# Second attention of a two-layer encoder step: biased scores written to on-chip memory, and unread products on the matrix engine

## The chip, the cores and the metric

The kernel runs on one core of a Trainium2 chip. What is compared is the device time of one execution in microseconds (us), from the runs of the kernel before and of the changed kernel on the same chip. Five engines work side by side and meet only through semaphores: TensorE (PE in the profile, PEld for its weight loads), VectorE (DVE), ScalarE (ACT), GpSimd (POOL) and SyncE (SP, which starts the transfers). Each engine takes its own instructions in the order in which the program lists them.

## The reference, cut to what matters

Two layers are computed for 512 prompt tokens and 32 sample tokens (544 columns together). Each layer projects its normalised input, runs two groups of attention heads, projects their outputs, and ends with a gated feed-forward part. The change touches the second attention alone ("B"): 8 heads of width 64; each query looks only at keys chosen by an indexer, with a bias by relative position.

```python
logits = jnp.einsum('bqhd,bqkhd->bqhk', qb, ks).astype(jnp.float32) * dh ** -0.5
bias = rel_bias[t5_bucket(sel_pos - pb[None, :, None])].astype(jnp.float32)
logits = logits + jnp.swapaxes(bias, 2, 3)
logits = jnp.where(valid[:, :, None, :], logits, -jnp.inf)
p = jax.nn.softmax(logits, axis=-1)
return jnp.einsum('bqhk,bqkhd->bqhd', p.astype(vs.dtype), vs)
...
x = x + jnp.concatenate([o_a.reshape(B, T, WIDTH_A), o_b.reshape(B, T, WIDTH_B)], axis=-1) @ w_out
```

The kernel computes full score rows and pushes the keys that were not chosen far below with an added mask.

## The kernel before, in words

Activations lie with features on the partitions and the 544 tokens along the free axis. Every weight block of 128 columns (a "unit", such as `bk` 3: keys of the second attention, head pair 3) is multiplied by TensorE in two halves of 24 products each (`("G", kind, i, 0)` and `("G", kind, i, 1)`, lines 1171, 1172 and 1175: weights and activations are each split in a high and a low part, three products per pair, 272 columns a product). ScalarE makes the high part of a unit (L887) as soon as the unit two before it is multiplied, and GpSimd then makes the low part (L1690).

One list of steps, written out by `layer_steps`, `a_phase` and `b_phase`, is walked by every engine; each engine executes what is its own in each step, in the order of the list. The second attention has 34 tiles of scores: for each of the four head pairs, four blocks of 128 queries (128, 256, 384, 512 keys wide) and two heads, then two tiles for the sample tokens. Two tiles make a pair, and step j of `b_phase` (j from 0 to 17) holds, in this order:

- `BL j`: TensorE writes the scores of pair j to two banks of its accumulator memory (PSUM), `a_ps[0]` and `a_ps[1]` (L1371; L1373 adds the mask). VectorE adds the bias in place and takes the row maxima (L1666), and negates them (L1668). Semaphore `b_max` says that a tile's maximum is there.
- `BX`: ScalarE takes the exponentials from `a_ps` into `prob` in on-chip memory (SBUF), with the row sums (L1020). Semaphore `b_exp`.
- work that fills the step: `N` (sums of squares for the key or query norm, L1210, read by VectorE at L1454), `Y` and `M` (the reciprocal root on ScalarE and VectorE), `W` (the normed queries or keys, L1498 and L1509 to L1511), `T` (transposes for the outputs), `G` (the next units: `bk`, `bq`, `bv`, and in steps 13 and 15 the first halves of the output projection, `wo` 0 and 1), `BR` (VectorE inverts the sums, L1673; GpSimd scales the probabilities, L1704; semaphore `b_nrm`).
- `BV p` in steps 5, 9, 13, 17: the product with the values for head pair p, into `a_ps[3]` (L691). VectorE copies the result out (L760).
- `BT`, one step late: TensorE transposes the two tiles of pair j-1 into `a_ps[2]` (both tiles, for the two narrow blocks) or into `a_ps[2]` and `a_ps[3]` (L1388; semaphore `bt_full`), and ScalarE copies them to `wts` and `work` (L1038, L1040; semaphore `bt_out`). On ScalarE these copies stand behind the exponentials of pair j.
- on VectorE then part of the top-k search of the sample tokens (L734, L737), or from step 9 the split of the first attention's output (`O`, L1051 and L1679).

After step 17 follow `BV s` (L1402, 24 narrow products for the sample tokens), the `O` steps 4 to 7, and the second half of `wo` 0 (`("G", "wo", 0, 1)`), which waits for them.

Two waits order the scores on TensorE in the kernel before: `BL j` waits until the exponentials of pair j-1 are done, since those still read `a_ps[0]` and `a_ps[1]`:

```python
pe.wait_ge(b_exp.sem, b_exp.at(l, btiles[2 * j - 1]))
```

and where a head pair begins (j = 4, 8, 12), also until `W` has written its keys. On ScalarE each exponential waits for the transposes (`bt_full`) of the tile four before, whose place in `prob` it takes.

Of the kernel before, what the change touches and what calls it, by code (L numbers as in the profile page):

```python
# [33 lines left out]
ALU = mybir.AluOpType  # L34
ACT = mybir.ActivationFunctionType
# [9 lines left out]
KT = DM // P  # L45
PAIRS = NH // 2
QB = SEQ // P
# [68 lines left out]
    return [("G", kind, i, 0), ("G", kind, i, 1)]  # L116


B_TILES = [(2 * p + e, b) for p in range(PAIRS) for b in range(QB) for e in range(2)] + [("s", 0), ("s", 1)]


# [42 lines left out]
def b_phase():  # L164


    n = len(B_TILES) // 2
    first, half, after = ({j: [] for j in range(n + 1)} for _ in range(3))
    for q in range(PAIRS - 1):
        p, j = q + 1, QB * q  # L170
        k = product("bk", p)
        first[j] += [("N", "bq", p), ("BR", j), ("Y", "bq", p), ("M", "bq", p)]
        half[j] += [k[0]] if q else []
        after[j] += [("W", "bq", p)]
        first[j + 1] += [("BR", j + 1)]
        half[j + 1] += [k[1], ("E", "bk", p)]
        after[j + 1] += [("S", "bk", p)]
        first[j + 2] += [("N", "bk", p), ("BR", j + 2), ("Y", "bk", p), ("M", "bk", p)]
        first[j + 3] += [("T", "bk", p - 1), ("BR", j + 3), ("W", "bk", p)]
        if p < PAIRS - 1:  # L180
            later = product("bq", p + 1)
            half[j + 2] += [later[0]]
            half[j + 3] += [later[1], ("E", "bq", p + 1)]
            after[j + 3] += [("S", "bq", p + 1)]
    last = QB * (PAIRS - 1)
    value = product("bv", PAIRS - 1)
    half[last - 1] += [value[0]]
    half[last] += [value[1], ("E", "bv", PAIRS - 1)]
    first[last] += [("T", "bk", PAIRS - 1)]
    first[last + 1] += [("T", "bv", PAIRS - 1)]  # L190
    half[last + 1] += [("G", "wo", 0, 0)]
    half[last + 3] += [("G", "wo", 1, 0)]
    for j in range(last, n):
        first[j] += [("BR", j)]
    for j in range(9):
        after[j] += [("TOPK", 1)]
    for j in range(KT // 2):
        after[9 + j // 2] += [("O", j)]
    s = []
    for j in range(n + 1):  # L200
        if j < n:
            s += [("BL", j), ("BX", 2 * j), ("BX", 2 * j + 1)]
        s += first[j] + half[j]
        if j >= 2 and B_TILES[2 * j - 4][1] == QB - 1:
            s += [("BV", (j - 2) // QB)]
        if j:
            s += [("BT", 2 * j - 2), ("BT", 2 * j - 1)]
        s += after[j]
    s += [("BV", "s")]
    return s  # L210


# [92 lines left out]
def trunk(nc, io, out):  # L305
# [31 lines left out]
    with ctx:  # L337
# [531 lines left out]
        def _(act):  # L869
# [8 lines left out]
            for l, st in steps:  # L878
# [135 lines left out]
                elif k == "BX":  # L1014
                    i = st[1]
                    w = b_width(btiles[i])
                    act.wait_ge(b_max.sem, b_max.at(l, btiles[i]))
                    if i >= 4:
                        act.wait_ge(bt_full.sem, bt_full.at(l, btiles[i - 4]))
                    act.activation(prob[:, i % 4, 0:w], a_ps[i % 2][:, 0:w], ACT.Exp,  # L1020
                                   bias=stat[:, i % 4, 1:2], accum_out=stat[:, i % 4, 2:3]).then_inc(b_exp.sem, 1)
                elif k == "BT":

# [88 lines left out]
        def _(pe):  # L1112
# [15 lines left out]
            for l, st in steps:  # L1128
# [65 lines left out]
                elif k == "R":  # L1194

                    if st[1] == 1:
                        if l:
                            pe.wait_ge(g_free[2].sem, g_free[2].last(l, slot_last[(2, l - 1)]))
                        pe.wait_ge(sqx_done.sem, sqx_done.at(l, st))
                    else:  # L1200
                        pe.wait_ge(b_exp.sem, b_exp.at(l, btiles[-1]))
                        pe.wait_ge(sqx_done.sem, sqx_done.at(l, st))
                    for a in range(2):
                        mm = pe.matmul(a_ps[a][:, 0:HALF], ones, sq[:, 1, a * HALF:(a + 1) * HALF], start=True, stop=True)
# [107 lines left out]
                elif k in ("ASZ", "ASS", "ASV"):  # L1312
# [22 lines left out]
                    else:  # L1335
# [3 lines left out]
                        for p in range(PAIRS):  # L1339
                            for kb in range(SKB):  # L1340
                                r, o = (P, kb * 256) if kb < 2 else (DEC, 512)
                                mm = pe.matmul(a_ps[3][:, p * 64:(p + 1) * 64], vs_nat["a"][0:r, kb, p * P:(p + 1) * P], wts[0:r, o + p * 64:o + (p + 1) * 64],
                                               start=(kb == 0), stop=(kb == SKB - 1))
                        mm.then_inc(o_full.sem, 1)
                elif k == "BL":
                    j = st[1]
                    pair = btiles[2 * j:2 * j + 2]
# [2 lines left out]
                    if j == 0:  # L1350
                        pe.wait_ge(a_w.sem, a_w.at(l, "s"))
                    else:
                        pe.wait_ge(b_exp.sem, b_exp.at(l, btiles[2 * j - 1]))
                    if (0, 1) in pair:
                        pe.wait_ge(tk_done.sem, tk_done.at(l, "p"))
                    if pair[0][0] == "s":
# [51 lines left out]
        def _(dve):  # L1408
# [13 lines left out]
            for l, st in steps:  # L1422
# [233 lines left out]
                elif k == "BL":  # L1656
                    for i in (2 * st[1], 2 * st[1] + 1):
                        t = btiles[i]
                        w = b_width(t)
                        dve.wait_ge(bl_full.sem, bl_full.at(l, t))  # L1660
                        if i >= 4:
                            dve.wait_ge(b_nrm.sem, b_nrm.at(l, btiles[i - 4]))
                        elif l:
                            dve.wait_ge(b_nrm.sem, b_nrm.last(l, btiles[i - 4]))
                        bias = bias_s[:, t[1], :] if t[0] == "s" else strip[:, t[0], SEQ - w:SEQ]
                        dve.tensor_tensor_reduce(a_ps[i % 2][:, 0:w], a_ps[i % 2][:, 0:w], bias, 1.0, TAKEN, ALU.add, ALU.max, stat[:, i % 4, 0:1])  # L1666
                        dve.drain()
                        dve.tensor_scalar(stat[:, i % 4, 1:2], stat[:, i % 4, 0:1], -1.0, None, ALU.mult).then_inc(b_max.sem, 1)  # L1668
                elif k == "BR":
# [79 lines left out]
```

## Time and profile before

| | |
|---|---|
| median of 3 runs | 1685.29 us (1685.22 to 1686.87) |
| profiled execution, its own time | 1682.84 us |
| span of its instructions | 1681.1 us |
| TensorE busy, share of the span | 94% (1586.4 us) |
| VectorE, ScalarE, GpSimd busy | 57%, 41%, 38% |
| mean granted TensorE clock | 0.984 of full speed |

The span runs from the first to the last instruction of the profiled execution; 1.74 us of its own time lie around it. The profile gives, for every instruction, its start and duration, and in brackets how long its engine had idled before it and what ended that. The granted clock is the share of full speed that TensorE had in a stretch; it is 1.00 (2.4 GHz) or 0.50 (1.2 GHz) at each moment. The second attention runs from about 275.6 to 399.5 us in the first layer, and from about 1098.1 to 1218.9 us in the second.

### The profile page before, as it was taken

The page shows a single profiled execution, that of the slowest core. Times are in us where ns is not written, and L with a number is a line of the kernel's source. Part 1 is how long each engine was busy: PE and PEld are TensorE (multiplying, and loading weights), DVE is VectorE, ACT ScalarE, POOL GpSimd, SP SyncE. Part 2 cuts the span into 40 slices and gives each one's busy share as a digit, 9 for nine tenths or more (in the row PEclk, how much of TensorE's full clock was granted, in tenths as well). Part 3 has the DMA queues.
Part 4 walks back from the last instruction along what each step waited for, and adds up shares of the span by engine and source line. Part 5 has one row for each costly group of instructions (what it writes and reads, how often), then busy time and mean ns, then how long its engine had stood idle before and what let it go on. Part 6 is the DMA issues. An engine that isn't in the chain of part 4 may idle for free.

```text
span 1681.1 us, 29872 instructions
## 1 busy us (share of the span) xinstructions
PE 1586.4 (94%) x11754; PEld 1467.2 (87%) x11762; DVE 966.3 (57%) x1764; ACT 683.6 (41%) x1296; POOL 631.6 (38%) x346
## 2 busy tenths in 40 slices
PE   6999998888999999999999999988799999999998
PEld 5788886767999999999987888866699999999998
DVE  6657757753666336516767667666366661662461
ACT  4335453543344234314433354535334431442342
POOL 5223332323643434333552333223264433334432
PEclk9999999998999999999999999999999999999999
DMA  6322211120322333333233322111122333323233
GB/s 187 90 85 84 70 40 38 52 66 26 88 83 82 88 89 89 88 89 89 74 90 109 93 58 58 43 41 45 53 66 87 89 86 91 89 83 89 81 89 94
DMA packets 242178, 131.43 MB, mean 78 GB/s; under 512 B 10302, under 2 KB 236590, under 8 KB 242038
## 3 DMA queue, kind: packets, MB, share of 16 engines
q1 hardware_dynamic: 242038, 129.52, 27.1%
q8 instruction: 93, 1.52, 0.4%
q14 instruction: 47, 0.39, 0.1%
HBM read 117.59 MB, written 11.62 MB: 77 GB/s over the span
## 4 chain that ended last, share of the span: by engine, by line
PE 70%; DVE 14%; ACT 6%; issue 3%; DVEq 3%; POOL 2%; ACTq 1%; DMA 0%; SPq 0%
PE g_ps L1171 13%; PE g_ps L1172 12%; PE g_ps L1175 12%; PE a_ps L1172 7%; PE a_ps L1171 7%; PE a_ps L1175 7%; DVE score L737 1%; ACT work L980 1%; PE a_ps L1264 1%; POOL w_lo L1690 1%; PE a_ps L1250 1%; DVE a_ps L1666 1%; DVE top L734 1%; PE a_ps L691 1%; ACT w_hi L887 1%
## 5 line engine op out<-in xcount | busy, mean ns | idle before, releaser
L1690 POOL TENSOR_TENSOR w_lo<-raw,w_hi 128x1024 fp32r<-128x1024 f32 (+2 forms) x210 | 504.9, 2404 | 712.5 <-ACT w_hi L887 712.5
L1171 PE MATMUL g_ps<-h_hi,w_hi 128*128 128x272 f32 (+1 forms) x1616 | 450.2, 296 | 8.9 <-DVEq L1573 2.9
L1172 PE MATMUL g_ps<-h_lo,w_hi 128*128 128x272 f32 (+1 forms) x1616 | 438.7, 290 | 0.0
L887 ACT ACTIVATE w_hi<-raw 128x1024 fp32r<-128x1024 f32 (+2 forms) x210 | 217.3, 1035 | 453.8 <-PE g_ps L1175 316.7
L1175 PE MATMUL g_ps<-h_hi,w_lo 128*128 128x272 f32 (+1 forms) x1616 | 336.7, 290 | 0.0
L1171 PEld LDWEIGHTS g_ps<-h_hi,w_hi 128*128 128x128 f32 (+1 forms) x1616 | 305.9, 189 | 22.9 <-issue 10.8
L1172 PEld LDWEIGHTS g_ps<-h_lo,w_hi 128*128 128x128 f32 (+1 forms) x1616 | 305.5, 189 | 1.3 <-issue 0.5
L1582 DVE SCALAR_TENSOR_TENSOR wts<-work,par,wts 128x546 f32<-128x546 f32 x176 | 201.5, 1145 | 99.3 <-ACT wts L1064 92.2
L1175 PEld LDWEIGHTS g_ps<-h_hi,w_lo 128*128 128x128 f32 (+1 forms) x1616 | 254.1, 189 | 0.0
L1171 PE MATMUL a_ps<-h_hi,w_hi 128*128 128x272 f32 x720 | 194.7, 288 | 0.0
L1172 PE MATMUL a_ps<-h_lo,w_hi 128*128 128x272 f32 x720 | 194.4, 289 | 0.0
L1175 PE MATMUL a_ps<-h_hi,w_lo 128*128 128x272 f32 x720 | 149.3, 288 | 0.0
L1171 PEld LDWEIGHTS a_ps<-h_hi,w_hi 128*128 128x128 f32 x720 | 135.6, 188 | 0.0
L1172 PEld LDWEIGHTS a_ps<-h_lo,w_hi 128*128 128x128 f32 x720 | 135.5, 188 | 0.0
L1175 PEld LDWEIGHTS a_ps<-h_hi,w_lo 128*128 128x128 f32 x720 | 112.6, 188 | 0.0
L1171 PE MATMUL g_ps<-act_hi,w_hi 128*128 128x272 f32 x364 | 99.3, 291 | 5.1 <-DVEq L1595 3.7
L1704 POOL TENSOR_SCALAR prob<-prob,stat 128x128 f32<-128x128 f32 (+4 forms) x68 | 38.3, 576 | 166.5 <-DVE stat L1673 166.5
L1064 ACT ACTIVATE wts<-work,par 128x546 f32<-128x546 f32 x88 | 74.4, 845 | 60.9 <-DVEq L643 59.4
L1172 PE MATMUL g_ps<-act_lo,w_hi 128*128 128x272 f32 x364 | 98.2, 289 | 0.0
L1171 PE MATMUL a_ps<-act_hi,w_hi 128*128 128x272 f32 x340 | 92.2, 289 | 0.9 <-POOL w_lo L1690 0.9
L1559 DVE TENSOR_TENSOR x_t<-x_t,g_ps 128x544 f32<-128x544 f32 x41 | 29.6, 721 | 108.5 <-PE g_ps L1175 107.8
L1172 PE MATMUL a_ps<-act_lo,w_hi 128*128 128x272 f32 x340 | 91.8, 289 | 0.0
(236 smaller groups left out, 2796.7 us busy)
## 6 DMA issues: line engine op xcount, KB each, us to landing
raw<-in_w_up SPq DMA_DIRECT2D x88, 512.0 KB, 3.8
raw<-in_w_in SPq DMA_DIRECT2D x56, 512.0 KB, 3.9
raw<-in_w_down SPq DMA_DIRECT2D x32, 512.0 KB, 3.8
raw<-in_w_out SPq DMA_DIRECT2D x16, 512.0 KB, 3.8
raw<-in_w_down SPq DMA_DIRECT2D x16, 384.0 KB, 3.4
x_nat<-in_x_prompt SPq DMA_DIRECT2D x4, 512.0 KB, 6.0
strip<-bias_line SPq DMA_DIRECT2D x8, 256.0 KB
out_p_av<-v_nat SPq DMA_DIRECT2D x4, 512.0 KB, 5.5
```

What stands on the lines that cost most here:

```text
L691: mm = pe.matmul(a_ps[3][d, c * P:SEQ], v_nat[:, c, p * P + e * HD:p * P + (e + 1) * HD], pair_weights(w, e, c), start=(c == 0), stop=(c = ...
L734: dve.max(top8[0:n, i, :], s)
L737: dve.match_replace(s, top8[0:n, i, :], s, TAKEN)
L887: act.activation(w_hi[:, n % SPLIT, 0:kt, 0:c], raw[:, n % RAW, 0:kt, 0:c], ACT.Copy).then_inc(hi_done, 1)
L1064: act.activation(cbuf[kind], ubuf[kind][:, 2:U], ACT.Identity, bias=par[:, 3, col:col + 1], scale=par[:, 2, col:col + 1]).then_inc(c_tap.s ...
L1171: pe.matmul(g[0:c, a, 0:HALF], w_hi[:, s, j, 0:c], xh[:, mov], start=(j == 0), stop=False)
L1172: pe.matmul(g[0:c, a, 0:HALF], w_hi[:, s, j, 0:c], xl[:, mov], start=False, stop=False)
L1175: mm = pe.matmul(g[0:c, a, 0:HALF], w_lo[:, s, j, 0:c], xh[:, mov], start=False, stop=(j == kt - 1))
L1559: dve.tensor_tensor(halves(x_t[:, m, :]), halves(x_t[:, m, :]), g, ALU.add)
L1582: dve.scalar_tensor_tensor(c, u[:, tap:tap + U - 2], par[:, tap, col:col + 1], c, ALU.mult, ALU.add)
L1690: pool.tensor_tensor(w_lo[:, s, 0:kt, 0:c], raw[:, n % RAW, 0:kt, 0:c], w_hi[:, s, 0:kt, 0:c].bitcast(F32), ALU.subtract).then_inc(lo_done, 1)
L1704: pool.tensor_scalar(prob[:, i % 4, 0:w], prob[:, i % 4, 0:w], stat[:, i % 4, 3:4], 1.0, ALU.mult, ALU.mult).then_inc(b_nrm.sem, 1)
```

## The change

The biased scores go from VectorE to `prob` in SBUF instead of back to `a_ps`, and the exponentials work in place there. So `BL j` waits for the maxima of pair j-1 and no more for their exponentials; the wait for the transposes of four tiles before moves from ScalarE's exponential to VectorE's first instruction on the tile. Second, six new steps `Z` per layer issue products of 128x512 on TensorE that nobody reads: 10, 4, 4, 10 and 3 of them ahead of `BL` 1, 8, 11, 12 and 15, 4 ahead of `BV s` and 6 behind it, 41 per layer. The first five write `a_ps[3]`, and so wait until ScalarE has copied out pair j-2 (`bt_out`; not at j = 1) and VectorE the last result from that bank (`o_out`); the other two write `a_ps[0]` and wait for the last maximum.

```diff
+FILL = {1: 10, 8: 4, 11: 4, 12: 10, 15: 3}
+FILL_END, FILL_OUT = 4, 6
...
     for j in range(n + 1):
+        if j in FILL:
+            s += [("Z", FILL[j], j)]
         if j < n:
             s += [("BL", j), ("BX", 2 * j), ("BX", 2 * j + 1)]
...
-    s += [("BV", "s")]
+    s += [("Z", FILL_END, n), ("BV", "s"), ("Z", FILL_OUT, n)]
...
                     act.wait_ge(b_max.sem, b_max.at(l, btiles[i]))
-                    if i >= 4:
-                        act.wait_ge(bt_full.sem, bt_full.at(l, btiles[i - 4]))
-                    act.activation(prob[:, i % 4, 0:w], a_ps[i % 2][:, 0:w], ACT.Exp,
+                    act.activation(prob[:, i % 4, 0:w], prob[:, i % 4, 0:w], ACT.Exp,
...
-                        pe.wait_ge(b_exp.sem, b_exp.at(l, btiles[-1]))
+                        pe.wait_ge(b_max.sem, b_max.at(l, btiles[-1]))
...
+                elif k == "Z":
+                    j = st[2]
+                    if j < len(btiles) // 2:
+                        if j >= 2:
+                            pe.wait_ge(bt_out.sem, bt_out.at(l, btiles[2 * j - 3]))
+                        pe.wait_ge(o_out.sem, o_out.at(l, ("b", (j - 6) // QB) if j >= 6 else ("a", "s")))
+                        idle = a_ps[3]
+                    else:
+                        pe.wait_ge(b_max.sem, b_max.at(l, btiles[-1]))
+                        idle = a_ps[0]
+                    for _ in range(st[1]):
+                        pe.matmul(idle[:, 0:SEQ], neg_ones_r, h_hi[:, 0, 0:SEQ], start=True, stop=True)
...
-                        pe.wait_ge(b_exp.sem, b_exp.at(l, btiles[2 * j - 1]))
+                        pe.wait_ge(b_max.sem, b_max.at(l, btiles[2 * j - 1]))
...
                         if i >= 4:
-                            dve.wait_ge(b_nrm.sem, b_nrm.at(l, btiles[i - 4]))
-                        elif l:
-                            dve.wait_ge(b_nrm.sem, b_nrm.last(l, btiles[i - 4]))
+                            dve.wait_ge(bt_full.sem, bt_full.at(l, btiles[i - 4]))
+                        else:
+                            dve.wait_ge(x_split.sem, x_split.at(l, ("X", 1, KT - 1)))
+                            if l:
+                                dve.wait_ge(b_nrm.sem, b_nrm.last(l, btiles[i - 4]))
...
-                        dve.tensor_tensor_reduce(a_ps[i % 2][:, 0:w], a_ps[i % 2][:, 0:w], bias, 1.0, TAKEN, ALU.add, ALU.max, stat[:, i % 4, 0:1])
+                        dve.tensor_tensor_reduce(prob[:, i % 4, 0:w], a_ps[i % 2][:, 0:w], bias, 1.0, TAKEN, ALU.add, ALU.max, stat[:, i % 4, 0:1])
```

## Rows read from the trace of the kernel before

**Rows 1.** Busy time by stretch, PE, PEld, DVE, ACT, POOL (instructions), granted clock, DMA

```profile
276.00:356.00 80.00, 65.89 (x430) 51.91 (x431) 57.21 (x157) 39.21 (x98) 23.71 (x27) 0.94 0.15 41
329.00:335.00 6.00, 5.24 (x20) 4.35 (x21) 3.60 (x13) 3.73 (x10) 3.68 (x4) 0.50 0.46 131
397.00:407.00 10.00, 7.84 (x34) 7.42 (x34) 3.35 (x7) 2.38 (x5) 0.00 (x0) 0.50 0.00 0
```

**Rows 2.** Waits of TensorE, first layer, second attention: us in total, times, longest

```profile
PE a_ps L1371 <- ACT prob L1020: 9.9, 4, 4.6
```

**Rows 3.** Timeline of VectorE, first layer: start, duration, instruction, idle before it

```profile
285.00 0.43 DVE L1666 CUSTOM_DVE_ANT_0 a_ps<-a_ps,strip 128x256 f32<-128x256 f32 x1
...
333.07 0.72 DVE L1454 TENSOR_SCALAR va<-g_ps 128x544 f32<-128x544 f32 x1 [0.54 <-PE g_ps L1210]
...
344.39 0.69 DVE L760 COPY o_t<-a_ps 128x512 f32<-128x512 f32 x1 [0.87 <-PE a_ps L691]
...
355.42 0.69 DVE L1666 CUSTOM_DVE_ANT_0 a_ps<-a_ps,strip 128x512 f32<-128x512 f32 x1
```

**Rows 4.** Timeline of TensorE, first layer, steps 8 to 12

```profile
329.18 0.80 PE L1371 MATMUL a_ps<-k_t,q_t 64*128 64x128 f32 x4 [2.82 <-DVEq L1512]
...
330.88 2.15 PE L1210 MATMUL g_ps<-sq,cf 128*128 128x272 f32 x4 [0.57 <-ACT sq L914]
...
350.05 1.13 PE L1371 MATMUL a_ps<-k_t,q_t 64*128 64x512 f32 x4 [2.58 <-ACT prob L1020]
...
355.10 0.82 PE L1388 MATMUL a_ps<-cf,prob 128*128 128x128 f32 x6
...
359.87 0.80 PE L1371 MATMUL a_ps<-k_t,q_t 64*128 64x128 f32 x4 [3.95 <-DVEq L1512]
...
366.83 1.04 PE L1388 MATMUL a_ps<-cf,prob 128*128 128x128 f32 x8
```

**Rows 5.** Timeline of ScalarE, first layer: last copies of transposed pairs 6, 9, 10, 13

```profile
329.70 0.48 ACT L1038 ACTIVATE work<-a_ps 128x384 f32<-128x384 f32 x1
...
351.53 0.38 ACT L1038 ACTIVATE work<-a_ps 128x256 f32<-128x256 f32 x1
...
359.38 0.48 ACT L1038 ACTIVATE work<-a_ps 128x384 f32<-128x384 f32 x1
...
378.79 0.38 ACT L1038 ACTIVATE work<-a_ps 128x256 f32<-128x256 f32 x1
```

**Rows 6.** Chain of waits, step 12: start, time of two products of 272 columns

```profile
364.34 0.45 PE g_ps L1175 x2
...
366.74 0.25 PE g_ps L1175 x2
```

**Rows 7.** Groups by line and shape: exponentials from SBUF and from PSUM, busy us, mean ns

```profile
L978 ACT ACTIVATE work<-work 128x512 f32<-128x512 f32 x32 | 20.0, 624 | 67.4 <-DVE work L1632 67.4
...
L1001 ACT ACTIVATE wts<-a_ps 128x512 f32<-128x512 f32 x16 | 8.7, 596 | 3.5 <-PE a_ps L1291 2.2 <-issue 1.3
```

**Rows 8.** Timeline of TensorE, first layer, step 15 and the end of the attention

```profile
378.68 1.13 PE L1371 MATMUL a_ps<-k_t,q_t 64*128 64x512 f32 x4 [1.90 <-ACT prob L1020]
...
384.75 0.82 PE L1388 MATMUL a_ps<-cf,prob 128*128 128x128 f32 x6
...
394.22 4.63 PE L1402 MATMUL a_ps<-wts,vsb 128*128 128x64 f32 x24 [0.62 <-ACT wts L1031]
...
401.01 0.59 PE L1171 MATMUL g_ps<-act_lo,w_hi 128*128 128x272 f32 x1 [2.16 <-DVE act_hi L1679]
```

**Rows 9.** Timeline of TensorE, second layer, steps 12 and 15

```profile
1182.24 0.80 PE L1371 MATMUL a_ps<-k_t,q_t 64*128 64x128 f32 x4 [3.60 <-DVEq L1512]
...
1187.79 1.03 PE L1388 MATMUL a_ps<-cf,prob 128*128 128x128 f32 x8
...
1199.63 1.13 PE L1371 MATMUL a_ps<-k_t,q_t 64*128 64x512 f32 x4 [1.90 <-ACT prob L1020]
...
1204.15 0.81 PE L1388 MATMUL a_ps<-cf,prob 128*128 128x128 f32 x6
```

## The prediction

> **What bounds the kernel now.** I read four kinds of view, in this order. The first is busy time by stretch. From 276 to 356 us VectorE is busy 57.21 of 80 us and TensorE's products do not fill the stretch; TensorE ran there at 0.94 of full speed, at half speed in single stretches such as 329 to 335 us and 397 to 407 us [rows 1]. So the second attention is a run of hand-overs, and TensorE's waits in it are only worth something where TensorE is what the others wait for.
>
> Second, TensorE's waits. The wait that the first edit removes, for the exponentials ahead of `BL`, costs 9.9 us in four places per layer, 4.6 us the longest [rows 2]. That looks like a prize. The third view, VectorE's timeline, shows that up to step 11 it is mostly none: the long wait is ahead of `BL` 2, because VectorE reaches the scores of `BL` 1 only at 285.00 [rows 3], after root, norm and top-k work, long after TensorE had written them. The scores of `BL` 11 are ready about 1.6 us after 350.05 [rows 4], and VectorE takes them at 355.42 [rows 3]. From step 12 it is TensorE's work that others wait for, up to `wo`.
>
> Fourth, the timelines of TensorE and ScalarE side by side, for the moment at which each fill may begin. A fill `Z` at step j stands in front of `BL j` and waits for ScalarE's copy of pair j-2; ScalarE makes that copy behind the exponentials of pair j-1. So wherever there is a fill with j of 2 or more, `BL` waits for more than in the kernel before, not for less. The copies end at 330.18, 351.91, 359.86 and 379.17 (start plus duration, [rows 5]), and the `BL`s behind them began at 329.18, 350.05 and 359.87 [rows 4] and 378.68 [rows 8]. The fill begins at 8, 11 and 15 after the old `BL` had begun, at 12 when it began. It does not fill the idle time; it comes behind it.
>
> **The change part by part.** One fill product has 512 columns. Two products of 272 columns took 0.45 us at half clock and 0.25 us at full clock [rows 6], so I take 512/272 of 0.225 and of 0.125: 0.42 us and 0.235 us.
>
> The ten products ahead of `BL` 1 (2.35 us) push `BL` 1 and the key product behind it by about 1.3 us. VectorE takes these scores only at 285.00 [rows 3], so I price them at 0; without that cover they would cost 1.3 us.
>
> Exponentials from SBUF: 512 columns take 624 ns from SBUF and 596 ns from PSUM [rows 7], 28 ns more; once per step on the chain that is 0.5 us per layer at most. The store by VectorE: 544 columns from PSUM to SBUF took 0.72 us, which makes 0.68 us for 512, against 0.69 us for the instruction of today [rows 3]; 68 tiles by 0.01 us give back 0.7 us at most. I take 0 for both together, with 1 us to either side. VectorE's new wait for the transposes of pair j-2 is covered: TensorE does them before it starts `BL j` at all. The shorter wait of `BL` in steps without a fill is worth 0 for the reason above (up to step 10) or because TensorE does not wait there (13, 14, 16).
>
> Step 8. TensorE has been idle since 326.36 (2.82 us before 329.18, [rows 4]) and the clock is at half [rows 1]. Fill from 330.18, four by 0.42, to 331.9: `BL` 8 is 2.7 us late. Behind it on TensorE stands `N`, which before began 1.70 us after `BL` 8 with 0.57 us of it waiting [rows 4]: now 331.9 + 1.13 + 2.15 = 335.2. VectorE, which took it at 333.07 [rows 3], is 2.1 us late. Slack: VectorE later waits 0.87 us for the value product [rows 3], and TensorE gets back about 1.5 us as the products that ran at half clock until 335 now run after that. Both come out 1.2 us late in step 9.
>
> Step 11. Copies at 351.91 + 1.2 = 353.1. TensorE, done at 347.47 + 1.2, has then idled 4.4 us, more than the waits of 2.82 and 3.95 us after which it ran at half clock; I take half: 1.7 us, `BL` 11 at 354.8 instead of 350.05. From there to the transposes `BT` of pair 10 it took 5.05 us at full clock [rows 4]; with the first 2 to 3 us of work at half clock 6 to 7, so 361.4. Transposes and copies (0.8 and 0.9 us) end at about 363.
>
> Step 12. Ten products at full clock, since TensorE was busy right before: 363 + 2.35 = 365.3 for `BL` 12 instead of 359.87. What it gains: from `BL` 12 to the next `BT` took 6.96 us in the first layer [rows 4], with 24 products at half clock, 0.1 us too long each; at full clock 4.5 us. `BT` at 369.8 instead of 366.83: 3.0 us late. In the second layer the same stretch took only 5.55 us [rows 9], so 5.4 + 4.5 - 5.55 = 4.4 us late, if the steps before repeat.
>
> Step 15. Copies end 0.5 us after the old `BL` 15, three products take 0.7 us: 1.2 us late (1.8 at half clock). From `BL` 15 to the next `BT` took 6.07 us in the first layer [rows 8] and 4.52 us in the second [rows 9]; the idle time ahead is longer now, so I take the middle, 5.3, for both: 1.2 - 0.8 = 0.4 us and 1.2 + 0.8 = 2.0 us. Sums so far: 3.4 and 6.4 us late.
>
> The end. Four products ahead of `BV s` take 0.94 us where 0.62 us were idle, 0.3 us late; six behind it lie in the 2.16 us in which TensorE waits for `wo` 0's operands [rows 8]. What they may give back is the clock: 7.84 us of TensorE's work in 397 to 407 ran at half speed [rows 1], so 3.9 us at most, 3.6 net. If the clock falls all the same, six products at half clock take 2.5 us, 0.4 us past the idle time: 0.7 us lost. I take the middle, 1.5 us gained per layer, since nothing in the trace shows such a mixture.
>
> The sum is 3.4 + 6.4 - 3.0 = 6.8, some 7 us. On the profiled execution's own 1682.84 us (span 1681.1 and 1.74 around it) that is 1689.8; the median of the runs lies 2.45 us above that execution, so 1692.3.
>
> Rows 4 show a wait of 2.58 us ahead of `BL` 11 with full-clock work behind it, and 2.82 us ahead of `BL` 8 with half-clock work behind it. The Trainium skill ("TensorE: Matmul & The Clock Gate", section "Why this matters for your kernels") advises to keep TensorE continuously busy and free of idle gaps, since the clock falls in them. Taken as a promise that fills hold the clock, it gives the first rival's sum; by the rows, fills that begin after the gap do not close it.
>
> **The rivals.**
> The fills hold the clock (the other side: faster). Its place is the restart after each gap; it decides if the products run at 0.235 us. Then fill 8 costs 0.94 us, `N` takes half of 2.15, and VectorE is 0.3 us late, which its 0.87 us of waiting covers. Fill 11 ends at 352.9; `BL` 11's scores are there before 355.42, and `BT` comes at 357.9, before the copies could start. Fill 12 ends at 362.2, `BT` at 366.7: -0.1 us in the first layer, +1.3 in the second. Step 15: 1.2 - 1.55 = -0.35 and +1.2. The end: -3.6 twice. Together -4.0 and -1.1: 1680.2 us. For it: such dense products are TensorE's heaviest work, and in step 12 of the second layer the clock came back sooner than in the first. Against it: the gaps ahead of 8 and 11 grow from 2.82 to 3.8 us and from 2.58 to 4.4 us.
>
> It balances: the fills are late as in my sum, but the end keeps the full clock in both layers: 9.8 - 7.2 = +2.6, or 1687.9 us.
>
> The change does what it says with the scores: `BL` no more waits for exponentials. Four places by some 0.7 us would be 5.6 us in both layers, 1679.7 us. Against it: at `BL` 1 and 2 VectorE is what is late, and at 11 and 15 a fill with a later wait stands in front.
>
> **How the numbers follow.** My forecast gets 0.57, the held clock 0.20, the balance 0.20, the scores 0.03. A measurement of this kernel can tell about 0.2% (3.4 us) from no change. Faster: held clock less the part of it that stays within 3.4 us, plus scores, 0.22; same: 0.20; slower: 0.58. The likeliest one's own range is 1689 to 1698: its upper end adds 1 us for each layer's step 11, 0.6 us twice for half-clock fills at step 15 and the loss at the end. The range over the cases, with one in ten left out on each side, is 1681 to 1698.
>
> **What would show it.** In the profile after: `BL` 8 at about 2.7 us past its old place relative to the norm before it, with the fill's products ahead of it at 0.42 us; `N` of step 8 still at 2.15 us; ScalarE's copy as what ends TensorE's idle time ahead of fills 8, 11, 12 and 15; `BL` 12 some 5 us later than before, with full-clock products behind it; `BV s` and `wo` 0 at full clock in some layer. I am wrong if fill products at 8 and 11 run at 0.235 us, if `wo` 0 starts earlier than before relative to the attention's start, or if the exponentials in place are dearer by 0.1 us or more.

## The result, and the profile after

The changed kernel takes 1688.93 us (median of 20 runs, 1685.54 to 1693.94); the kernel before takes 1682.05 us on the same chip (20 runs, 1678.15 to 1686.87). The ratio is 1.0042, with a 95% interval of 1.0033 to 1.005: slower by 6.9 us. The sum in the prediction was +6.8 us. Its 1692.3 us lies 3.4 us above the measured time: 3.2 us of that because it was added to the median of the three runs shown at first, 1685.29 us, where twenty runs give 1682.05, and 0.2 us because 6.8 was rounded up to 7.

The profiled execution after has a span of 1686.4 us against 1681.1. Of these 5.3 us, 1.7 us were there before the changed attention of the first layer began (its first scores start at 277.31 instead of 275.60; TensorE ran at a granted clock of 0.66 from 49 to 54 us, where the other execution had 1.00). No instruction is changed up to there, so that belongs to the execution, not to the change. Places below are therefore counted from the first `BL` of their layer: 277.31 and 1097.68 after, 275.60 and 1098.07 before.

Busy time by stretch, columns as in [rows 1]:

```profile
276.00:356.00 80.00, 67.91 (x423) 53.10 (x424) 54.66 (x156) 40.05 (x98) 23.70 (x27) 0.92 0.15 41
397.00:407.00 10.00, 9.42 (x64) 8.28 (x63) 3.93 (x7) 3.10 (x5) 0.00 (x0) 1.00 0.01 2
```

TensorE is busier than in [rows 1] (67.91 against 65.89 us), and VectorE less (54.66 against 57.21). The end now runs at full clock (1.00 instead of 0.50).

The waits of TensorE in the first layer's attention, as in [rows 2]; the third line is of the kernel before, which waited there for its keys (`W`) too:

```profile
PE a_ps L1359 <- ACT work L1041: 10.4, 4, 4.5
PE a_ps L1386 <- DVE stat L1685: 2.6, 1, 2.6
...
PE a_ps L1371 <- DVEq L1512: 7.7, 3, 4.0
```

The 9.9 us of waiting for exponentials are gone. In their place stand 10.4 us in which a fill (L1359) waits for ScalarE's copy (L1041), again in four places, the longest of 4.5 us, and 2.6 us for maxima ahead of `BL` 2. Ahead of the scores TensorE idled 17.6 us before (9.9 and, for keys, 7.7) and 13.0 us now; but the five fills take 9.2 us, so idle time and fills together are 22.2 us ahead of the scores, where 17.6 us stood before. The fills have not used up the idle time; most of it stands in front of them.

TensorE in steps 8 to 12, first layer, to be read against [rows 4]:

```profile
331.54 1.20 PE L1359 MATMUL a_ps<-h_hi,cr 128*128 128x512 f32 x4 [2.84 <-ACT work L1041]
332.67 0.49 PE L1386 MATMUL a_ps<-k_t,q_t 64*128 64x128 f32 x4
333.21 2.06 PE L1213 MATMUL g_ps<-sq,cf 128*128 128x272 f32 x4
...
353.79 2.08 PE L1359 MATMUL a_ps<-h_hi,cr 128*128 128x512 f32 x4 [4.53 <-ACT work L1041]
355.80 1.79 PE L1386 MATMUL a_ps<-k_t,q_t 64*128 64x512 f32 x4
...
361.52 0.82 PE L1403 MATMUL a_ps<-cf,prob 128*128 128x128 f32 x6
362.97 2.60 PE L1359 MATMUL a_ps<-h_hi,cr 128*128 128x512 f32 x10 [0.63 <-ACT work L1041]
365.50 0.49 PE L1386 MATMUL a_ps<-k_t,q_t 64*128 64x128 f32 x4
...
369.62 1.03 PE L1403 MATMUL a_ps<-cf,prob 128*128 128x128 f32 x8
```

The copies of ScalarE for which these fills waited, as in [rows 5]:

```profile
331.00 0.48 ACT L1041 ACTIVATE work<-a_ps 128x384 f32<-128x384 f32 x1
...
353.36 0.38 ACT L1041 ACTIVATE work<-a_ps 128x256 f32<-128x256 f32 x1
...
362.44 0.48 ACT L1041 ACTIVATE work<-a_ps 128x384 f32<-128x384 f32 x1
...
381.47 0.37 ACT L1041 ACTIVATE work<-a_ps 128x256 f32<-128x256 f32 x1
```

Each of these fills begins 0.05 to 0.06 us after its copy ends (331.48, 353.74, 362.92 and 381.84). None begins where the idle time begins; the idle times of 2.84 and 4.53 us stay whole, and the products come behind them. Counted from the first `BL`, `BL` 8 is 1.8 us later than in [rows 4], `BL` 11 4.0 us and `BL` 12 3.9 us. Two readings of the clock: the four products at 331.54 took 1.13 us until `BL`, 0.28 each, at full clock, and it fell behind them, in the norm (2.06 us, as 2.15 before). The four at 353.79 ran at half clock, 0.50 each. In step 12 the clock held (ten products in 2.53 us, 0.25 each), and from `BL` 12 to the next transposes TensorE took 4.1 us instead of the 6.96 of [rows 4]: `BT` comes 1.1 us late, not 3.9.

Step 15 and the end, first layer, against [rows 8]:

```profile
381.90 0.97 PE L1359 MATMUL a_ps<-h_hi,cr 128*128 128x512 f32 x3 [2.36 <-ACT work L1041]
382.79 1.13 PE L1386 MATMUL a_ps<-k_t,q_t 64*128 64x512 f32 x4
...
387.32 0.82 PE L1403 MATMUL a_ps<-cf,prob 128*128 128x128 f32 x6
...
395.90 1.18 PE L1359 MATMUL a_ps<-h_hi,cr 128*128 128x512 f32 x4
396.92 3.76 PE L1417 MATMUL a_ps<-wts,vsb 128*128 128x64 f32 x24
400.60 1.66 PE L1359 MATMUL a_ps<-h_hi,cr 128*128 128x512 f32 x6
402.84 0.39 PE L1174 MATMUL g_ps<-act_lo,w_hi 128*128 128x272 f32 x1 [0.58 <-DVE act_hi L1696]
```

`BV s` takes 3.76 instead of 4.63 us, and the second half of `wo` 0 starts with 0.58 us of waiting instead of 2.16, its first product 0.39 us long instead of 0.59. By `wo` 2 this attention is 2.4 us ahead of the one before (410.29 less 277.31, against 411.00 less 275.60).

The second layer, against [rows 9]:

```profile
1175.54 2.08 PE L1359 MATMUL a_ps<-h_hi,cr 128*128 128x512 f32 x4 [5.38 <-ACT work L1041]
...
1187.63 0.49 PE L1386 MATMUL a_ps<-k_t,q_t 64*128 64x128 f32 x4
...
1191.74 0.49 PE L1403 MATMUL a_ps<-cf,prob 128*128 128x128 f32 x3
...
1204.03 1.65 PE L1359 MATMUL a_ps<-h_hi,cr 128*128 128x512 f32 x3 [2.36 <-ACT work L1041]
1205.61 2.08 PE L1386 MATMUL a_ps<-k_t,q_t 64*128 64x512 f32 x4
...
1212.39 0.82 PE L1403 MATMUL a_ps<-cf,prob 128*128 128x128 f32 x6
```

Here the clock stood at half from the first product of the fill of step 15 (1.65 us for three products; granted 0.50 from 1204 to 1210 us): the transposes behind it start 8.6 us later than before, counted from the first `BL`. `wo` 2 comes 5.1 us late in this layer (1235.35 less 1097.68, against 1230.60 less 1098.07). One execution shows where fills start, but where the clock falls differs between the two layers of one kernel. What each part is worth is therefore taken from the timed runs below.

Groups by line and shape: the products of the fills, then the exponential of 512 columns and the second part of the scores instruction (which hands over the maximum), each after (L1023, L1683) and before (L1020, L1666):

```profile
L1359 PE MATMUL a_ps<-h_hi,cr 128*128 128x512 f32 x82 | 26.0, 456 | 21.9 <-ACT work L1041 21.9
L1023 ACT ACTIVATE prob<-prob,stat 128x512 f32<-128x512 f32 x16 | 11.6, 723 | 28.8 <-DVE stat L1685 27.9
L1020 ACT ACTIVATE prob<-a_ps,stat 128x512 f32<-128x512 f32 x16 | 11.0, 688 | 25.9 <-DVE stat L1668 25.9
L1683 DVE DVE_READ_ACCUMULATOR2_ANT stat<- 128x1 f32 x68 | 5.6, 82 | 0.0
L1666 DVE DVE_READ_ACCUMULATOR2_ANT stat<- 128x1 f32 x68 | 9.5, 140 | 0.0
```

### The profile page after: what moved, and what is told of

It is laid out like the page before. It is cut to its first block, busy times and chain, and to the rows that moved or that the text cites. A ratio compares the mean times of both kernels' runs of the same rounds, so it can differ in the third digit from the quotient of the medians.

```text
span 1686.4 us, 29996 instructions
## 1 busy us (share of the span) xinstructions
PE 1604.4 (95%) x11844; PEld 1476.1 (88%) x11844; DVE 964.1 (57%) x1764; ACT 686.1 (41%) x1296; POOL 631.8 (37%) x346
## 4 chain that ended last, share of the span: by engine, by line
PE 73%; DVE 12%; ACT 6%; issue 3%; DVEq 2%; POOL 2%; ACTq 1%; DMA 0%; SPq 0%
PE g_ps L1174 13%; PE g_ps L1175 13%; PE g_ps L1178 13%; PE a_ps L1175 7%; PE a_ps L1174 7%; PE a_ps L1178 7%; PE a_ps L1267 2%; POOL w_lo L1707 1%; PE a_ps L1253 1%; PE a_ps L696 1%; DVE score L742 1%; ACT work L985 1%; DVE prob L1683 1%; ACT w_hi L892 1%; DVE top L739 1%
```

## The experiments

Twelve kernels, each timed beside the kernel before in one of four groups. The median of the kernel before was 1681.38 us in the first group (`e1` to `e4`), 1681.11 in the second (`e5` to `e8`), 1681.61 in the third (`e9` to `e11`) and 1681.91 in the last (`e12`). The difference is to the kernel before of the same group. The intervals are 1.4 to 3.4 us to either side, so a difference of two such differences is good to 3 to 4 us. In the table the numbers behind "late" and "early" are the steps that keep a fill: a late fill has the waits of the changed kernel, an early one waits for the maxima only (`e9_sized` differs, see there). "End" stands for the two fills beside `BV s`.

| kernel | median, us | difference, us | ratio, 95% interval |
|---|---|---|---|
| changed kernel | 1688.93 | +6.9 | 1.0042 (1.0033 to 1.005) |
| `e1_scores`: scores edit, no fills | 1677.05 | -4.3 | 0.997 (0.996 to 0.998) |
| `e2_end`: scores, end fills | 1673.87 | -7.5 | 0.9954 (0.9939 to 0.997) |
| `e3_steps`: scores, step fills | 1694.37 | +13.0 | 1.0077 (1.0057 to 1.0097) |
| `e4_early`: all, step fills early | 1673.00 | -8.4 | 0.995 (0.9935 to 0.9964) |
| `e5_no_11_15`: late 1, 8, 12, end | 1680.66 | -0.5 | 0.9995 (0.9984 to 1.0005) |
| `e6_only_11_15`: late 11, 15, end | 1681.02 | -0.1 | 0.9995 (0.9985 to 1.0006) |
| `e7_wait_exp`: scores, old wait | 1680.96 | -0.2 | 0.9998 (0.9984 to 1.0012) |
| `e8_one_late`: one product per step fill | 1677.96 | -3.2 | 0.9977 (0.9965 to 0.9988) |
| `e9_sized`: early, longer, six steps | 1673.87 | -7.7 | 0.9953 (0.9939 to 0.9968) |
| `e10_1_8`: late 1, 8, end | 1678.25 | -3.4 | 0.9981 (0.9968 to 0.9993) |
| `e11_early_1_8_12`: early 1, 8, 12, end | 1669.68 | -11.9 | 0.993 (0.9914 to 0.9945) |
| `e12_only_1`: fill 1, end | 1673.84 | -8.1 | 0.9958 (0.9944 to 0.9971) |

The theory from the prediction: the cost is that the fills of steps 8 to 15 start behind ScalarE's copy and push `BL`. The rivals: the scores edit itself is dear; the products themselves are the cost, wherever they stand.

**The parts one by one.** `e1_scores`:

```diff
-FILL = {1: 10, 8: 4, 11: 4, 12: 10, 15: 3}
-FILL_END, FILL_OUT = 4, 6
+FILL = {}
+FILL_END, FILL_OUT = 0, 0
```

> The scores edit alone, with no fill product at all: scores in SBUF, exponentials in place, BL waits for the maxima. Theory 1 (the cost is that the fills of steps 8 to 15 start behind ScalarE's copy and push BL): the edit by itself is within 1.7 us of the kernel before (ratio 0.999 to 1.001), because VectorE is what is late ahead of BL 2 and the wait for the exponentials ended early elsewhere. Theory 2 (the scores edit itself is dear: exponentials longer, VectorE's new wait for the transposes): slower by about 7 us, 1.004. Theory 3 (the removed wait was worth what the profile lists): faster by 5 to 6 us, 0.9967.

It is faster by 4.3 us, outside the first theory's 1.7 us and near the third's 5 to 6, which its interval (3.4 to 6.7 us) holds: the removed wait is worth something, as long as no fill stands in front of `BL`. The second theory is excluded.

`e2_end` keeps only the fills at the end:

```diff
-FILL = {1: 10, 8: 4, 11: 4, 12: 10, 15: 3}
+FILL = {}
```

> The scores edit and only the fills at the end (4 ahead of BV s, 6 behind it); none in the steps. Theory 1: these two stand in time that TensorE idled, keep BV s and the start of wo 0 at full clock and give 2 to 3.5 us per layer: faster by 3 to 7 us, ratio 0.996 to 0.998. Rival (the end is paced by the splits of the first attention's output and by GpSimd's low parts of wo, so the clock there is worth nothing): within 1.7 us of the scores edit alone.

It is 7.5 us faster than the kernel before, 3.2 us more than the scores edit alone. So here the end gives about 1.6 us per layer, where the prediction took 1.5. By itself that is hardly clear of the rival (within 1.7 us of the scores edit); but beside the step fills the same end fills give 6.1 us (`e3_steps`, next), and with both the rival falls. The end does not hold the clock in every layer. In the first layer of this kernel the six products ran at half clock:

```profile
393.30 2.93 PE L1359 MATMUL a_ps<-h_hi,cr 128*128 128x512 f32 x6
```

`e3_steps` keeps only the fills in the steps:

```diff
-FILL_END, FILL_OUT = 4, 6
+FILL_END, FILL_OUT = 0, 0
```

> The scores edit and only the fills of steps 1, 8, 11, 12 and 15; none at the end. Theory 1: this carries the whole loss, 9 to 13 us slower than before, ratio 1.0055 to 1.008 (the changed kernel's 7 us and what the end gives back). Rival (the fills are harmless and the scores edit costs 7 us): 1.004 as for the changed kernel.

It is 13.0 us slower than before, at the upper end of the first theory, and 17.3 us slower than the scores edit alone. With the end fills in both kernels (changed kernel against `e2_end`) the same fills cost 14.4 us. The whole loss is theirs.

**Place or length.** `e4_early` leaves every count and takes away the late wait: the scores no longer stay in PSUM, so the first bank is free as soon as the maxima are taken, and that is what `BL` waits for anyway.

```diff
-                        if j >= 2:
-                            pe.wait_ge(bt_out.sem, bt_out.at(l, btiles[2 * j - 3]))
-                        pe.wait_ge(o_out.sem, o_out.at(l, ("b", (j - 6) // QB) if j >= 6 else ("a", "s")))
-                        idle = a_ps[3]
+                        pe.wait_ge(b_max.sem, b_max.at(l, btiles[2 * j - 1]))
+                        idle = a_ps[0]
```

> All fills in the same numbers, but those of the steps write the bank that BL is about to overwrite, and wait for nothing but the maxima that BL waits for itself: the late wait for ScalarE's copy is gone, the length stays. Theory 1 (what costs is where the fill may begin, not its 41 products): the fills fall into the idle time, BL is late by 1 us at most, the clock stays up through steps 8 to 16, and the kernel is faster than before by 3 to 10 us, ratio 0.994 to 0.998. Rival (the products themselves are the cost, 31 in the steps at 0.26 us are 8 us per layer in front of BL): 1.003 to 1.006, as the changed kernel or worse.

The same 31 products per layer now cost nothing in sum: 0.9 us faster than `e2_end`, and 15.3 us faster than the changed kernel. That is the theory's outcome. The wait and the bank that is written change together, and no run separates them; that the late wait costs by itself is shown next.

`e8_one_late` does the opposite: the late wait stays, the length goes.

```diff
-FILL = {1: 10, 8: 4, 11: 4, 12: 10, 15: 3}
+FILL = {1: 1, 8: 1, 11: 1, 12: 1, 15: 1}
```

> The changed kernel with one product instead of 10, 4, 4, 10 and 3 in the fills of the steps, the waits and the end unchanged: the late start stays, the length goes. Theory A (the wait for the copy is the cost): 8 to 14 us over scores with end fills alone, 1682 to 1688 us, ratio 1.000 to 1.004. Rival B (the length is): 1 to 3 us over it, 1675 to 1677 us, 0.996 to 0.9975.

Both theories of that expectation miss: it costs 4.4 us over `e2_end`, between the 1 to 3 and the 8 to 14. So the late wait with one product is some 4.4 of the 14.4 us, and the other 26 products per layer, behind that wait, are 10.0 us. Nine of these 26 stand at step 1, which has no late wait and costs nothing (`e12_only_1`, below); over the other 17, in two layers, that is 0.29 us each, about the length of a product. The theory in its strong form (the wait alone) falls. What holds is the sum of the two, as the prediction priced it: where a fill begins late, its length is on the path; where it begins early (`e4_early`), most of it is not. The rows of step 11 show the wait by itself:

```profile
350.82 0.51 PE L1359 MATMUL a_ps<-h_hi,cr 128*128 128x512 f32 x1 [4.38 <-ACT work L1041]
351.26 2.08 PE L1386 MATMUL a_ps<-k_t,q_t 64*128 64x512 f32 x4
```

TensorE idles 4.38 us, and `BL` 11 (2.08 us for four products) runs at half clock as it does behind four fill products.

**Which fill.** `e5_no_11_15` and `e6_only_11_15` split them:

```diff
-FILL = {1: 10, 8: 4, 11: 4, 12: 10, 15: 3}
+FILL = {1: 10, 8: 4, 12: 10}
```

> The changed kernel without the fills of steps 11 and 15 (late fills of 10, 4 and 10 products stay at 1, 8 and 12, and both at the end). The steps' fills together cost 15 us (changed kernel against scores with end fills alone). Theory A (the fills at 11 and 15 carry it, because there BL would otherwise start at the maxima, long before the copy): 1673 to 1678 us, ratio 0.995 to 0.998. Rival B (it is spread over the fills by their products, 24 of 31 remain, 11.6 us): 1.001 to 1.003.

```diff
-FILL = {1: 10, 8: 4, 11: 4, 12: 10, 15: 3}
+FILL = {11: 4, 15: 3}
```

> The changed kernel with only the fills of steps 11 and 15 (4 and 3 products, late) and those at the end. Theory A: seven products carry nearly the whole loss, 1685 to 1690 us, ratio 1.002 to 1.005. Rival B (by products, 7 of 31, 3.5 us): 1676 to 1679 us, 0.997 to 0.999.

Neither expectation was right. The 24 products of 1, 8 and 12 cost 7.1 us over `e2_end`, the 7 products of 11 and 15 cost 7.4 us; the two add up to 14.5, the whole loss. By product, 11 and 15 are more than three times as dear, and still twice as dear if the ten at step 1 are left out. That fits with the scores edit: there `BL` would start at the maxima, and the fill puts the copy in front of it. In `e6_only_11_15` the trace shows how much of step 11 is given back at once (first layer):

```profile
355.12 2.08 PE L1359 MATMUL a_ps<-h_hi,cr 128*128 128x512 f32 x4 [4.55 <-ACT work L1041]
357.12 1.79 PE L1386 MATMUL a_ps<-k_t,q_t 64*128 64x512 f32 x4
...
362.85 0.82 PE L1403 MATMUL a_ps<-cf,prob 128*128 128x128 f32 x6
363.66 0.49 PE L1386 MATMUL a_ps<-k_t,q_t 64*128 64x128 f32 x4
```

`BL` 12 follows the transposes at once; in `e2_end` it waits 4.57 us for its keys there. Counted from the first `BL`, `BL` 11 is 6.5 us later than in `e2_end` and `BL` 12 only 2.5. A fill at 12 behind the copy uses up that slack again.

`e10_1_8` and `e12_only_1` take 12 and then 8 out of the late ones:

```diff
-FILL = {1: 10, 8: 4, 11: 4, 12: 10, 15: 3}
+FILL = {1: 10, 8: 4}
```

> The changed kernel with only the late fills of steps 1 and 8 (10 and 4 products) and those at the end. Late fills at 1, 8 and 12 cost 6.8 us over end fills alone (1673.9). Theory A (the fill at 12 carries it: ten products behind the copy, in front of BL 12): 1673 to 1676 us, ratio 0.995 to 0.997. Rival B (the fill at 8 carries it, 2.7 us of lateness per layer that is not absorbed): 1678 to 1681 us, 0.998 to 1.000.

```diff
-FILL = {1: 10, 8: 4, 11: 4, 12: 10, 15: 3}
+FILL = {1: 10}
```

> The changed kernel with the fill of step 1 alone (10 products, no late wait) and those at the end. The fills of 1 and 8 cost 4.4 us over end fills alone. Theory A (VectorE reaches the scores of BL 1 only later, so the ten products are hidden and the cost is step 8's late fill): 1672 to 1675.5 us, ratio 0.9945 to 0.9965. Rival B (the ten products push the key product behind BL 1, and the step's later work with it): 1676.5 to 1679 us, 0.997 to 0.9985.

The fill at 1 costs nothing (0.6 us less than `e2_end`), the fill at 8 4.7 us, the fill at 12 2.9 us, each good to 3 to 4 us; theory A of `e10_1_8` falls, that of `e12_only_1` holds. The ten products at 1 are the longest fill and free, four products at 8 are not. For step 8 the traces show less than the runs: in the profiled executions `BT` 14 comes 0.75 and 0.9 us later in `e10_1_8` than in `e12_only_1`, counted from the first `BL`; the rest of the 4.7 us stays open.

**What the scores edit is worth, and where.** `e7_wait_exp` is `e1_scores` with the old wait:

```diff
-                        pe.wait_ge(b_max.sem, b_max.at(l, btiles[2 * j - 1]))
+                        pe.wait_ge(b_exp.sem, b_exp.at(l, btiles[2 * j - 1]))
```

> The scores edit alone, without fills, but BL waits for the exponentials of the pair before, as in the kernel before, and not for the maxima. The scores edit alone was 4.3 us faster. Theory A (what it gained is the earlier BL, mostly at 11 and 15): this is back at the kernel before, ratio 0.999 to 1.001. Rival B (it gained on VectorE, whose second part of the scores instruction took 82 ns against 140 ns in 68 tiles, 3.9 us in all): the gain stays, 0.997 to 0.998.

The gain is gone (-0.2 us). So the 4.3 us are the earlier `BL`; the shorter scores instruction and the longer exponential come to nothing between them. Step 15 shows it, `e1_scores` first, then `e7_wait_exp`, second layer:

```profile
1196.68 0.60 PE L1403 MATMUL a_ps<-cf,prob 128*128 128x128 f32 x4
1198.35 1.13 PE L1386 MATMUL a_ps<-k_t,q_t 64*128 64x512 f32 x4 [1.08 <-DVE stat L1685]
```

```profile
1197.34 0.60 PE L1403 MATMUL a_ps<-cf,prob 128*128 128x128 f32 x4
1199.75 1.13 PE L1386 MATMUL a_ps<-k_t,q_t 64*128 64x512 f32 x4 [1.82 <-ACT prob L1023]
```

From the transposes to `BL` 15 it is 1.67 us instead of 2.41, 0.74 us in each layer. At step 11 the second layer of `e1_scores` needs 2.36 us from the transposes of pair 9 to `BL` 11, where the kernel before needs 3.20; its first layer shows no gain (3.38 against 3.18). In `e2_end`, with the same scores edit, it is 2.37 in both layers. How much of step 11 counts is not shown, since VectorE takes these scores later in any case ([rows 3]). Step 15 makes 1.5 of the 4.3 us; the rest isn't located.

**Better versions.** `e11_early_1_8_12` is `e4_early` without the fills at 11 and 15:

```diff
-FILL = {1: 10, 8: 4, 11: 4, 12: 10, 15: 3}
+FILL = {1: 10, 8: 4, 12: 10}
...
-                        if j >= 2:
-                            pe.wait_ge(bt_out.sem, bt_out.at(l, btiles[2 * j - 3]))
-                        pe.wait_ge(o_out.sem, o_out.at(l, ("b", (j - 6) // QB) if j >= 6 else ("a", "s")))
-                        idle = a_ps[3]
+                        pe.wait_ge(b_max.sem, b_max.at(l, btiles[2 * j - 1]))
+                        idle = a_ps[0]
```

> Early fills behind the maxima as before, but only at 1, 8 and 12 (10, 4, 10), none at 11 and 15, with the end fills. Theory A (the early fills of 11 and 15 stand behind the maxima in front of BL, whose scores VectorE waits for, and cost their length): 1 to 4 us faster than with them (1673.0), 1669 to 1672 us, ratio 0.993 to 0.995. Rival B (they cost nothing): 1672 to 1674 us.

It is the fastest of all, 1669.68 us, 11.9 us under the kernel before and 3.5 us under `e4_early` by their differences. The traces agree: counted from the first `BL`, the transposes behind `BL` 15 come 1.6 us earlier than in `e4_early` in the first layer and 2.1 us in the second. Steps 8 and 12 of its first layer:

```profile
326.74 0.82 PE L1401 MATMUL a_ps<-cf,prob 128*128 128x128 f32 x6
327.31 1.19 PE L1357 MATMUL a_ps<-h_hi,cr 128*128 128x512 f32 x4
329.37 0.49 PE L1384 MATMUL a_ps<-k_t,q_t 64*128 64x128 f32 x4 [0.87 <-DVEq L1525]
...
355.01 0.82 PE L1401 MATMUL a_ps<-cf,prob 128*128 128x128 f32 x6
356.35 2.59 PE L1357 MATMUL a_ps<-h_hi,cr 128*128 128x512 f32 x10 [0.52 <-DVE stat L1683]
358.87 0.49 PE L1384 MATMUL a_ps<-k_t,q_t 64*128 64x128 f32 x4
```

The fill of step 8 follows the transposes without a gap, and `BL` 8 waits another 0.87 us for its keys behind it: the four products are hidden.

`e9_sized` goes further and sizes the fills to the idle time:

```diff
-FILL = {1: 10, 8: 4, 11: 4, 12: 10, 15: 3}
+FILL = {1: 10, 2: 8, 8: 7, 11: 9, 12: 14, 15: 6}
...
-                        if j >= 2:
-                            pe.wait_ge(bt_out.sem, bt_out.at(l, btiles[2 * j - 3]))
-                        pe.wait_ge(o_out.sem, o_out.at(l, ("b", (j - 6) // QB) if j >= 6 else ("a", "s")))
-                        idle = a_ps[3]
+                        if j in (8, 12):
+                            pe.wait_ge(b_max.sem, b_max.at(l, btiles[2 * j - 1]))
+                            idle = a_ps[0]
+                        else:
+                            if j >= 11:
+                                pe.wait_ge(bt_out.sem, bt_out.at(l, btiles[2 * j - 7]))
+                            pe.wait_ge(o_out.sem, o_out.at(l, ("b", (j - 6) // QB) if j >= 6 else ("a", "s")))
+                            idle = a_ps[3]
```

> A version built from what the runs showed: the scores edit, the end fills, and fills in the steps that wait for nothing late and are sized to the idle time: 10, 8, 7, 9, 14 and 6 products at steps 1, 2, 8, 11, 12 and 15; those at 1, 2, 11 and 15 write the fourth bank and wait only for the last reader that this bank really had (the pairs two before are narrow and use the third bank alone), those at 8 and 12 write the first bank behind the maxima. Theory A (where idle time is filled from its beginning, the clock stays up and the work behind it is shorter): 1 to 5 us faster than the early fills of 10, 4, 4, 10 and 3, so 1668 to 1672 us, ratio 0.992 to 0.995. Rival B (VectorE and ScalarE set the pace of the steps, so a held clock there is worth nothing): 1671 to 1675 us, 0.994 to 0.997, the same as end fills alone.

It is level with `e2_end` and 4.2 us behind `e11_early_1_8_12`, though TensorE's mean clock over its span is 0.992 against 0.986 for `e2_end`. That is the time of rival B, but the traces do not bear out its reason, that a held clock is worth nothing. These are the stretches from `BL` 12 to `wo` 2, columns as in [rows 1]: first layer of the kernel before, of `e2_end`, `e9_sized` and `e11_early_1_8_12`, then second layer of `e2_end` and `e9_sized`.

```profile
359.87:411.00 51.13, 43.38 (x254) 35.04 (x255) 15.34 (x47) 19.09 (x51) 10.95 (x14) 0.80 0.14 44
358.64:404.84 46.20, 41.95 (x263) 33.26 (x265) 14.84 (x48) 19.65 (x53) 10.91 (x14) 0.89 0.15 48
363.08:408.12 45.04, 41.86 (x271) 33.02 (x271) 14.84 (x48) 19.67 (x52) 10.47 (x13) 0.92 0.13 43
358.87:401.46 42.59, 37.76 (x264) 29.30 (x265) 14.85 (x48) 19.68 (x52) 10.87 (x14) 1.00 0.16 52
...
1176.65:1221.59 44.94, 40.69 (x263) 32.02 (x265) 14.85 (x48) 19.67 (x53) 10.92 (x14) 0.92 0.16 50
1179.90:1222.74 42.84, 39.08 (x270) 30.31 (x271) 14.85 (x48) 19.67 (x52) 10.46 (x13) 1.00 0.14 46
```

Without a late fill in it, this stretch is the shorter the higher the granted clock: 51.13 us at 0.80, 42.59 us at 1.00. (The first layer of the changed kernel, with its late fill at 15, took 44.79 us at 1.00.) `e9_sized` runs through it 1.2 and 2.1 us faster than `e2_end`, but reaches `BL` 12 2.45 us later in the first layer (0.2 in the second): there the fourteen products outlast the idle time. In these executions the two roughly cancel. Which of its other fills cost what was not tried.

The Trainium skill ("TensorE: Matmul & The Clock Gate", section "Why this matters for your kernels") says that idle gaps between bursts of products should be avoided, or the clock falls. `e11_early_1_8_12` agrees: from `BL` 12 to `wo` 2 it had 1.00 in the first layer and 0.96 in the second, where the kernel before had 0.80 and 0.86. `e9_sized` shows the limit of the advice in this kernel: its clock is higher than that of `e2_end`, and its time is the same; by the stretches above, its fills push back the scores by about what the clock gives.

## Why the prediction was right

**The sum.** +6.8 us were predicted, +6.9 measured. By the runs: the scores edit -4.3, the end fills -3.2, the step fills +14.4. The prediction counted scores and step fills together against the kernel before, 3.4 + 6.4 = +9.8, and the end -3.0; the runs give +10.1 (14.4 less 4.3) and -3.2. Taken in the other order it is +13.0 (`e3_steps`) and -6.1, and that is the order of the prediction: steps and scores against the kernel before, the end on top of them. So each term was some 3 us too small, and the two misses cancel. 3 us is also what these differences are good to, so the runs cannot say which split is right; the signs and the order of size are the same both ways, but that the sum came out within 0.1 us is luck.

The profiled execution is nearer to another row of the prediction. Counted from the first `BL` to `wo` 2 it is 2.4 us ahead in the first layer and 5.1 us late in the second, +2.7 together, where the rival that balances has +2.6. It is one execution; the twenty runs (+5.6 to +8.4 by the interval) exclude that rival's time.

**Step 1.** Priced at 0, measured 0 within what the runs can tell (`e12_only_1`). The 1.3 us without cover should have been 1.5: TensorE idles 0.89 us ahead of `BL` 1 in the kernel before, and the products were taken at 2.35. Nothing hangs on it.

**The scores edit and the wait of `BL`.** The step held for this change: with a fill in front, `BL` waits for more than before, and the gain does not appear. Without fills the rival on the scores, which had a chance of 0.03 for the whole change, is real: 4.3 us, near its 5.6. So the shorter wait, priced at 0 in the steps without a fill, is worth something by itself; the changed kernel does not show it, since its fills stand at the places that count. The prediction placed it rightly at 11 and 15, and 11 and 15 are where the late fills take it away (7.4 us for seven products). The terms that it put at 0, exponentials in place and the store, do cancel (`e7_wait_exp`), though each was larger than taken: 35 ns instead of 28 for an exponential of 512, 65 ns instead of 10 for the scores' instructions (58 in the second part, and 691 against 698 in the first).

**Step 8.** `BL` 8 was to be 2.7 us late with products at half clock, 0.42 each; it was 1.8 and 3.5 us late, with products at full clock, 0.28 each. This sign was named as one that would make the prediction wrong, and at step 8 the step was wrong: the gap of 2.84 us did not put the fill at half clock, the clock fell just behind it, in the norm (first layer), or not there (second layer, 1.14 us). The idle time ahead of the fill was 2.84 and 3.18 us, not the 3.8 of the forecast. By `BT` 9 the lateness was 0.1 and 0.4 us against the kernel before, where 1.2 was forecast. The timed runs say otherwise (4.7 us for this fill in both layers, `e10_1_8` against `e12_only_1`); what the step costs stays open.

**Steps 11 and 12.** Here the steps came out as written: 4.53 us idle (4.4 forecast), half clock, `BL` 11 4.0 and 5.2 us late (4.75 forecast), `BL` 12 3.9 and 5.8 us late (5.4), with full clock behind it; `BT` 11 1.1 and 4.3 us late (3.0 and 4.4). Only the price of a product was too small: 0.50 instead of 0.42 us at half clock, 0.25 to 0.28 instead of 0.235 at full clock.

**Step 15.** By its `BT` the first layer was 0.9 us late (3.4 forecast), the second 8.6 (6.4): 9.5 together against 9.8. In this one execution the clock was at half in the fill of the second layer and not in that of the first, so two misses of more than 2 us cancel here too.

**The end.** 1.5 us per layer were forecast, the middle between a held clock and none. Without step fills it measured 1.6 (`e2_end` against `e1_scores`), with them 3.0 (changed kernel against `e3_steps`). In the profiled execution both layers kept the full clock, as in the rival that balances, and TensorE got from the transposes behind `BL` 15 to `wo` 2 3.3 and 3.5 us faster than before; in `e2_end` one layer did not keep it. The first rival (held clock everywhere, faster) needed fills that begin at the start of the gaps. Given those (`e4_early`), the kernel is 8.4 us faster than before.

## What to carry to other kernels

Before a filler is put into a stall, look at the moment at which its own operands and its target come free: one that waits for something later than the instruction behind it moves the stall in front of that instruction and adds its own length. Give it a target that is free for a reason which the next instruction waits for anyway; here that was worth 15 us. And put fillers only where the wait behind them is for another engine's work (the keys at steps 8 and 12): ahead of a product that others are waiting for, even an early filler costs (3.5 us at steps 11 and 15). A held clock pays where the others wait for TensorE, here from step 12 on, and the fillers that hold it must not push that work back by as much.

## What the runs showed of the hardware

A product of 512 columns that nobody reads took 0.25 to 0.28 us at full clock and 0.50 to 0.53 us at half clock, more than the columns scaled from products of 272 (0.235 and 0.42); each of them has a weight load of its own in the trace (82 for 82 products), although the weights are always the same. The second part of VectorE's scores instruction, which hands over the row maximum, took 82 ns when the scores went to SBUF and 140 ns when they went back to PSUM. The exponential of 512 columns took 723 ns in place in SBUF and 688 ns from PSUM.
